# A two-layer backbone kernel: text and image tokens separated at two norm stages

## The reference

```python
for l in range(2):
    h_lat = modulate(rms_norm(x, g0), sh1, sc1)            # image tokens
    h_ctx = modulate(rms_norm(x_ctx, g0), csh1, csc1)      # text tokens
    if l == 0: y_lat, y_ctx = attention(h_lat, h_ctx) @ w_out
    else:      y_lat, _     = gated_delta_rule(h_lat, h_ctx) @ w_out
    x = x + gt1 * rms_norm(y_lat, g1)
    h = modulate(rms_norm(x, g2), sh2, sc2)
    x = x + gt2 * rms_norm((silu(h @ w_gate) * (h @ w_up)) @ w_down, g3)
    if l == 0: ...the same two updates for x_ctx with y_ctx and its own sh, sc, gt...
```

## Time and profile before

| | us |
|---|---|
| runs (3), median | 1237.39 (1236.99 to 1237.61) |
| the profiled execution | 1236.43 |
| its span in the trace | 1234.7 |
| PE busy | 1169.0 (95%) |
| DVE busy | 616.0 (50%) |
| ACT busy | 564.1 (46%) |
| mean granted TensorE clock | 0.986 |

### The profile page before, as it was taken

How to read it: one execution, slowest core, us unless ns; L and a number is a source line. 1 busy time by engine, 2 the same in 40 slices (tenths; PEclk the granted TensorE clock), 3 DMA queues, 4 the chain that set the end, 5 groups by cost and what they waited for, 6 DMA issues and landing times.

```text
span 1234.7 us, 17661 instructions
## 1 busy us (share of the span) xinstructions
PE 1169.0 (95%) x6999; PEld 911.7 (74%) x6999; DVE 616.0 (50%) x973; ACT 564.1 (46%) x1061; POOL 121.2 (10%) x117
## 2 busy tenths in 40 slices
PE   6899989999899999999999889999979998999997
PEld 2577735468378888888888638788869976888886
DVE  2532258763543233333222276489986525666653
ACT  2622247764462223323222274866355535766642
POOL 0030320110001111111000000010015100111100
PEclk9899999999999999999999999999979999999999
DMA  9754656653553333333333462234203032766661
GB/s 345 222 163 143 181 181 228 205 138 87 159 146 102 92 96 102 93 95 94 94 94 97 148 154 76 69 84 111 62 18 86 5 102 69 205 187 187 186 191 68
DMA packets 222892, 159.51 MB, mean 129 GB/s; under 512 B 14794, under 2 KB 191324, under 8 KB 222812
## 3 DMA queue, kind: packets, MB, share of 16 engines
q1 hardware_dynamic: 222032, 158.11, 43.2%
q10 hardware_dynamic: 780, 0.29, 0.1%
HBM read 157.33 MB, written 1.05 MB: 128 GB/s over the span
## 4 chain that ended last, share of the span: by engine, by line
PE 80%; DVE 9%; ACT 6%; issue 2%; DMA 1%; SPq 1%; POOL 0%; DVEq 0%; ACTq 0%; POOLq 0%
PE bank L1409 44%; PE bank L1420 6%; PE bank L1591 5%; PE bank L1421 3%; PE bank L1396 2%; PE bank L1467 2%; PE bank L1663 2%; PE bank L1498 1%; ACT h_work L1788 1%; PE bank L1673 1%; DVE blocks L1046 1%; DVE outer L1044 1%; PE bank L804 1%; PE bank L1517 1%; PE bank L1694 1%
## 5 line engine op out<-in xcount | busy, mean ns | idle before, releaser
L1409 PE MATMUL bank<-h_both,w_hi 128*128 128x512 f32 x1296 | 404.0, 393 | 0.0
L2002 DVE TENSOR_TENSOR w_lo<-w_raw,w_hi 128x1024 fp32r<-128x1024 f32 (+1 forms) x161 | 201.9, 1254 | 235.4 <-ACT w_hi L1755 234.4
L1409 PEld LDWEIGHTS bank<-h_both,w_hi 128*128 128x128 f32 x1296 | 242.0, 188 | 51.1 <-issue 0.7
L1409 PE MATMUL bank<-h_both,w_lo 128*128 128x512 f32 x648 | 252.5, 390 | 0.0
L1755 ACT ACTIVATE w_hi<-w_raw 128x1024 fp32r<-128x1024 f32 (+1 forms) x161 | 167.2, 1040 | 81.1 <-PE bank L1409 57.0
L1409 PEld LDWEIGHTS bank<-h_both,w_lo 128*128 128x128 f32 x648 | 121.6, 188 | 25.6
L1421 PE MATMUL bank<-h_both,w_lo 128*128 128x256 f32 x308 | 86.5, 281 | 0.0
L1420 PE MATMUL bank<-h_both,w_hi 128*128 128x512 f32 x231 | 83.0, 398 | 1.4 <-DVE h_both L2059 1.0
L1409 PE MATMUL bank<-act_hi,w_hi 128*128 128x512 f32 x176 | 68.5, 389 | 0.0
L1409 PE MATMUL bank<-act_lo,w_hi 128*128 128x512 f32 x176 | 68.5, 389 | 0.0
L1409 PE MATMUL bank<-act_hi,w_lo 128*128 128x512 f32 x176 | 68.5, 389 | 0.0
(11 more groups left out here) (301 smaller groups left out, 1834.0 us busy)
## 6 DMA issues: line engine op xcount, KB each, us to landing
w_raw<-in_ada_w SPq DMA_DIRECT2D x96, 512.0 KB, 4.8
w_raw<-in_ffn_w_gate_up SPq DMA_DIRECT2D x88, 512.0 KB, 3.9
w_raw<-in_ffn_w_down SPq DMA_DIRECT2D x38, 512.0 KB, 3.8
w_raw<-in_gdn_w_in SPq DMA_DIRECT2D x32, 512.0 KB, 4.0
w_raw<-in_attn_w_in SPq DMA_DIRECT2D x14, 512.0 KB, 4.0
w_raw<-in_gdn_w_out SPq DMA_DIRECT2D x8, 512.0 KB, 5.2
w_raw<-in_ffn_w_down SPq DMA_DIRECT2D x8, 384.0 KB, 3.4
w_raw<-in_attn_w_in SPq DMA_DIRECT2D x8, 256.0 KB, 3.4
```

The costliest lines, as they stand in the source:

```text
L1409: m = nc.tensor.matmul(dst, stationary(a, k), moving(b, k), start=(first and k == kk[0] and a == b == 0), stop=(last and k == kk[-1] and a ...
L2002: nc.vector.tensor_tensor(w_lo[where[key] % N_RAW][:, 0:tiles, 0:w], raw_slot(key)[:, 0:tiles, 0:w], w_hi[hi_slot(m)][:, 0:tiles, 0:w].bit ...
```

## The change

The streams get separate jobs and semaphores at two places. The attention output is made in two passes over its 8 tiles, first the text columns, then the image columns, with the text stream's norms put among the image tiles; five gate tiles (`HELD`) are then made for text columns, and then for image columns, each on its own PSUM bank, the image stream's norms among the text half. The last down tile is made text first and then image, and three delta rule tiles (`DELTA_HELD`: ab, k0, k1) likewise. All matmuls at these places, the norms' too, have 256 columns in place of 512. The weights of the tiles that are held need places: five spare `w_hi` slots lie where `act_hi` and the attention buffers are unused. Of the 11 ada chunks behind attention and the 11 behind the down tiles, 12 go in pairs behind the gate tiles 8, 14, 20, 26, 32 and 38, and 10 (2, 4 and 4) stay behind the down tiles. Helpers named `..._part` and `..._held` do for one stream what `take_y`, `sum_y`, `post_norm` and `pre_norm` did for both; `square_part` and `pre_step` keep the ring of 4 squares. In the diff, cut to its core, the PE program comes first, then `down_held` and `out_held` of ACT and of DVE.

```diff
-GAP_COUNTS = (2, 3, 6)
-ADA_GAPS = {"gap0": 34 + 2 * len(ADA_UNITS), "gap1": 34 + 2 * len(ADA_UNITS) + sum(GAP_COUNTS)}
+GAP_COUNTS = (2, 4, 4)
+ADA_GATES = [8 + 6 * n for n in range(6)]
+ADA_GAPS = {"gap1": 34 + 2 * len(ADA_UNITS) + 2 * len(ADA_GATES)}
...
+    if phase == "gate0" and step in ADA_GATES:
+        return pair(34 + 2 * len(ADA_UNITS), ADA_GATES.index(step))
...
-    out += [("attout", m) for m in range(KT)] + [("ada", a) for a in gap("gap0")]
+    out += [("attout", m) for m in range(KT)]
...
+        w_hi += [at(f"w_hi_spare{n}", [KT, P], F32R, BIG + 16384 + 4096 * n) for n in range(5)]
...
+        SPARE = {split_no["attout", m]: N_SPLIT + 1 + m - 3 for m in range(3, KT)}
+        SPARE.update({split_no["gdn", "k", n]: N_SPLIT - 1 + n for n in range(2, 4)})
+        SPARE.update({split_no["gate", 0, n]: N_SPLIT + 1 + n - 3 for n in range(3, HELD + 2)})
+        hi_slots, hi_users, last_user, turns = [], [], {}, 0
+        for n in range(len(split_chunks)):
+            j = (n - LATE) % (N_SPLIT + 1)
+            if n in SPARE:
+                slot = SPARE[n]
+            elif n < LATE:
+                slot = turns % N_SPLIT
+                turns += 1
+            else:
+                slot = (turns + j) % N_SPLIT if j < N_SPLIT else N_SPLIT
+            hi_slots.append(slot)
+            hi_users.append(last_user.get(slot, None))
+            last_user[slot] = n
...
+                if n >= WHOLE_AT:
                     project_whole(key)
-                elif n > 1:
+                elif n >= DELTA_HELD:
...
-                for m in range(KT):
-                    project(("attout", m), ("y", 0, m), 0, there=None if m else heads_there)
+                for s in range(2):
+                    for m in range(KT):
+                        w, job = weights(("attout", m)), y_job(0, m, s)
+                        finish(three(take(job)[:, token_cols(s)], w,
+                                     lambda part, k: (h_hi, h_lo)[part][:, k, token_cols(s)],
+                                     range(KT), True, True, before=heads_there if m == s == 0 else None), job)
+                        if s and m == 0:
+                            post_part(0, 0)
+                        if s and m == 4:
+                            pre_part(1, 0)
+            def post_part(i, s):
+                pe.wait_ge(y_acc_parts[s], acc_no(i, KT - 1, s))
+                dst = take(post_job(i, s), "side")
+                finish(nc.tensor.matmul(dst[:, token_cols(s)], ones, post_views[i][2][:, token_cols(s)],
+                                        start=True, stop=True), post_job(i, s))
+            def pre_step(j, s, k):
+                if k == 0:
+                    take(pre_job(j, s), "side")
+                pe.wait_ge(sq_parts[s], norm_no(j, k, s))
+                m = nc.tensor.matmul(bank(pre_job(j, s))[:, token_cols(s)], ones, pre_sq[:, k % 4, token_cols(s)],
+                                     start=(k == 0), stop=(k == KT - 1))
+                finish(m, ("held_sq", j, s, k))
+                done_at[pre_job(j, s)] = jobs[0]
+            def pre_part(j, s):
+                for k in range(KT):
+                    pre_step(j, s, k)
+            def held_step(j, dsts, ws, s, k):
+                pe.wait_ge(h_parts[s], norm_no(j, k, s))
+                for key in dsts:
+                    width = dsts[key].shape[0]
+                    for a, b in ((0, 0), (0, 1), (1, 0)):
+                        m = nc.tensor.matmul(dsts[key][:, token_cols(s)], ws[key](a, k)[:, 0:width],
+                                             (h_hi, h_lo)[b][:, k, token_cols(s)],
+                                             start=(k == a == b == 0), stop=(k == KT - 1 and a == 1))
+                    if s and k == KT - 1:
+                        finish(m, key)
+            def gates_held():
+                held = [("gate", 0, n) for n in range(HELD)]
+                dsts, ws = {}, {}
+                for keys in [held[0:2]] + [[key] for key in held[2:]]:
+                    for key in keys:
+                        dsts[key], ws[key] = take(key), weights(key)
+                    for k in range(KT):
+                        held_step(1, {key: dsts[key] for key in keys}, ws, 0, k)
+                        if keys[0] == held[0] and k == 1:
+                            post_part(0, 1)
+                    if keys[0] == held[HELD - 2]:
+                        pre_part(1, 1)
+                for k in range(KT):
+                    held_step(1, dsts, ws, 1, k)
+            def delta_held():
+                held = [("gdn",) + GDN_STEPS[n] for n in range(DELTA_HELD)]
+                dsts = {key: take(key, "gdn")[0:chunk_shape(key)[1]] for key in held}
+                ws = {key: weights(key) for key in held}
+                for k in range(KT):
+                    held_step(2, dsts, ws, 0, k)
+                    if k >= 2:
+                        pre_step(2, 1, k - 2)
+                for k in range(KT - 2, KT):
+                    pre_step(2, 1, k)
+                for k in range(KT):
+                    held_step(2, dsts, ws, 1, k)
+            def last_down():
+                m = KT - 1
+                keys = [("down", 0, m, part) for part in range(len(DOWN_PARTS))]
+                ws = [weights(key) for key in keys]
+                for s in range(2):
+                    job = y_job(1, m, s)
+                    dst = take(job)[:, token_cols(s)]
+                    for part, (a, b) in enumerate(DOWN_PARTS):
+                        last = three(dst, lambda p, k: ws[part](p, k - a),
+                                     lambda p, k: (act_hi, act_lo)[p][:, k, token_cols(s)],
+                                     range(a, b), part == 0, part == len(DOWN_PARTS) - 1)
+                        finish(last, keys[part] if s else ("downc", m, part))
+                        if s and part == 0:
+                            post_part(1, 0)
+                    done_at[job] = jobs[0]
+                ada(ada_after("gap1", 0))
+                post_part(1, 1)
+                ada(ada_after("gap1", 1))
+                pre_part(2, 0)
+                ada(ada_after("gap1", 2))
...
-            ada(ada_after("gap0", 0))
-            post_norm(0)
-            ada(ada_after("gap0", 1))
-            pre_norm(1)
-            ada(ada_after("gap0", 2))
             ffn(0)
-            ada(ada_after("gap1", 0))
-            post_norm(1)
             if LAST_SUB == 3:
-                ada(ada_after("gap1", 1))
-                pre_norm(2)
-                ada(ada_after("gap1", 2))
+                delta_held()
...
+            def down_held():
+                take_part(1, KT - 1, 0)
+                post_part(1, 0)
+                for k in range(KT):
+                    square_part(2, k, 0)
+                    if k == 3:
+                        take_part(1, KT - 1, 1)
+                    if k == 5:
+                        post_part(1, 1)
+                first = split_no["gdn", "ab", 0]
+                split_to(first + 1)
+                pre_part(2, 0)
+                def squares(k):
+                    if k < KT:
+                        square_part(2, k, 1)
+                    if k == 0:
+                        split_to(first + 2)
+                h_part(2, 0, squares)
+                pre_part(2, 1)
+                def steps(k):
+                    if k in (4, 7):
+                        split_to(first + DELTA_HELD + k // 7)
+                h_part(2, 1, steps)
+            def out_held():
+                for m in range(KT):
+                    split_out(split_to, 0, m)
+                    take_part(0, m, 0)
+                take_part(0, 0, 1)
+                post_part(0, 0)
+                take_part(0, 1, 1)
+                for k in range(3):
+                    square_part(1, k, 0)
+                take_part(0, 2, 1)
+                for k in range(3, 4):
+                    square_part(1, k, 0)
+                split_gate(split_to, 0)
+                take_part(0, 3, 1)
+                take_part(0, 4, 1)
+                for k in range(4, KT):
+                    square_part(1, k, 0)
+                split_gate(split_to, 1)
+                pre_part(1, 0)
+                def other(k):
+                    if k in (1, 4, 7):
+                        take_part(0, 5 + k // 3, 1)
+                h_part(1, 0, other)
+                split_gate(split_to, 2)
+                post_part(0, 1)
+                split_gate(split_to, 3)
+                for k in range(KT):
+                    square_part(1, k, 1)
+                    if k == 3:
+                        split_gate(split_to, 4)
+                pre_part(1, 1)
+                def gates(k):
+                    if k == KT - 2:
+                        split_gate(split_to, HELD)
+                h_part(1, 1, gates)
+                split_gate(split_to, HELD + 1)
...
+            def down_held():
+                sum_part(1, KT - 1, 0)
+                def last_sum(k):
```

(51 more changed lines are left out.)

147 lines of the change are left out of this document (121 added, 26 removed).

## The result

The changed kernel takes 1251.03 us (median of 4 runs, 1250.5 to 1252.41), the kernel before beside it 1237.22 (4 runs, 1236.99 to 1237.61): a ratio of 1.0113, 95% interval 1.0098 to 1.0128. It is slower by 13.8 us, on the side that I forecast, but 11 us above the forecast and 6.5 above the range. The profiled executions stand further apart than the medians, 1252.41 against 1236.43 us.

The account below looks back on a forecast made before the run. PE's matmuls bound the kernel, except behind attention and the down tiles, where an ACT and DVE latency chain does. 1236.43 - 7.0 (attention, net) + 8.7 (down tiles) + 0.9 (clock) = 1239.0 profiled, 1240.0 us as median; range 1232.0 to 1244.5.

Parts of the forecast that it names:

- Clock: Behind attention and the down tiles: one fall to half clock loses 1.7 us; half of one was counted, 0.9 us.
- two falls 3.4: Clock case within the forecast's side: two falls, each over a PE-bound stretch, cost 3.4 us in place of 0.9, giving 1242.5.
- Work behind the down tiles: From the end of down tile 6 to `cum`, PE's work without waits was counted as 51.9 us.
- Waits behind the down tiles: From the end of down tile 6 to `cum`, seven listed PE waits were to come to 19.4 us together.
- the ring: Behind the down tiles: ACT's image squares 4 to 7 wait for PE's `pre_step` on the 4-deep ring; 1.5 us in all.
- ab's copy: Behind the down tiles: PE waits for the copy of ab before its transpose, 0.8 us.
- wait 3: Before the first held delta rule matmul, PE waits for late k0 and k1 DMAs, their copies and the text chain: 6.9 us.
- Behind attention: From attention's output tiles to the end of gate 4: gain of 12.9 us, with no PE wait over 1 us.
- Moved ada chunks: Twelve ada chunks moved between gate tiles, where PE is always busy: 6 pairs at 0.98 us, 5.9 us lost.
- Start: Attention's output tiles were taken to start at 274.44 us, as in the kernel before.
- its 7.8: Lower value of the loss behind the down tiles, with half-width matmuls at 0.1133 us instead of 0.118.
- The rival "faster": Behind the down tiles wait 3 is short, text h follows 5.5 us earlier and the clock stays up: 1233.6 us; chance 0.20.

Follow-up runs that it names:

- e3: Changed kernel plus idle matmuls, never read, ahead of TensorE's four long waits behind the down tiles; 1244.11 us.
- e5: Changed kernel with its half behind the down tiles undone and VectorE's order there as in the kernel before; 1228.98 us.
- e6: Changed kernel with five ada chunks run early on TensorE, ahead of the last down tile; 1251.39 us.
- e9: Changed kernel with the first three delta rule chunks right behind two ada chunks in SyncE's queue, and eight ada pairs among the gate tiles; 1252.20 us.
- e2: Changed kernel with attention's end put back as in the kernel before, streams parted only behind the down tiles; 1261.89 us.
- e12: Changed kernel with two delta rule tiles held, k1's copies in the image half, last down weights requested late, idle matmuls in two long waits; 1240.09 us.
- e10: Changed kernel with two delta rule tiles held instead of three, and k1's copies moved into the image half; 1244.84 us.

## Why the prediction was wrong

To the Gram start the loss is 810.63 - 795.64 = 15.0 us, the prediction's sum 8.7 + 0.9 - 7.0 = 2.6. The 12.4 us between, by its steps:

- **Clock: the step that failed, 8.4 us.** "I count half of one fall, 0.9 us" and "two falls 3.4" at worst. There were four stretches, 23.8 us, each behind a wait of 2.2 us or more; the work under them cost 9.3 us by the estimate above, 5.9 ahead of `cum` and 3.4 behind it. Filling the waits gave back 7.7 (e3). The prediction had a row of the kernel before with waits of up to 3 us at 1.00 and took it for a rule. But e5, with nearly the same waits in that place, falls there twice (706.9 and 720.5 us). It costs nothing there: from the end of tile 7 to `cum` e5 takes 46.6 us, and so does the kernel before, because ScalarE and VectorE lead. And the kernel before has a second fall behind attention, from 340.0 us, behind a wait of 2.5 us, which the prediction passed over (window, PE only):

```profile
340.00:342.00 2.00, 2.00 (x5) 0.50 1.10 286
```

- **Work behind the down tiles, 1.4 us.** Counted 51.9. PE is busy for 59.2 there; 5.9 of the difference are the half clock, 0.6 the spacing of 0.120 in place of 0.118. The other 0.8 I can't place.
- **Waits behind the down tiles, -1.0 us.** 18.4 against 19.4, each at its place: 3.3 (3.1), 8.5 (6.9), 3.4 before the image half (4.2 with k2's copy), 2.2 (2.4), 0.3 (0.5), 0.6 on the ring (1.5), and nothing for ab's copy (0.8). For wait 3 the prediction named both causes, the slots eight back and the order on ScalarE and VectorE; e6 and e9 show both, and that neither mends it alone. What it had not seen is that the queue hangs on the last down tile's held weights, not only on the ada chunks.
- **Behind attention, 1.5 us.** 84.4 us from attention's first tile to the end of gate 4, against 82.9: the spacing was at the upper bound or just over it (23.63/195 and 14.66/120, 0.121 and 0.122), and 624 x 0.002 = 1.2. (The prediction's own terms, 355.8 + 0.2 + 0.4 + 0.7, give 357.1 and not 357.3.) Gain 11.4 instead of 12.9. No wait over 1 us, as said.
- **Moved ada chunks, 1.4 us.** The 0.98 of the row is the piece; each pair also breaks the row of gate matmuls. 324.2 us less 1398 x 0.2267 leaves 7.3, or 1.22 a pair.
- **Start, 0.6 us.** Attention's tiles began at 275.04 in place of 274.44.

Together 12.3 of the 12.4 us. One of the prediction's bounds was also added up wrong, and moves nothing: 276 matmuls at 0.1133 save 1.3 us, so its 7.8 should be 7.4.

Behind the Gram start another 0.9 us came, with a longer half-clock stretch in the scan (17.1 us in place of 13.7). The forecast's side and its reason, more lost behind the down tiles than won behind attention, were right, and e5 and e2 show it: -3.9 and +20.4 us. The rival "faster" needed wait 3 to be short, and it was the longest.

The attention half alone, e5, beats both kernels: 1228.98 us, 22 less than the changed kernel and 9.0 less than the one before. With three repairs of its second half together (e12) the changed kernel stays 7.4 us behind e5 at the Gram start.

## What to carry to other kernels

Price a new wait of a matmul-bound engine twice: its length, and the matmuls behind it at half clock. Here four waits of 2.2 to 8.5 us cost 17 us by themselves, and filling them gave back 7.7 more. The second price is a risk and not a sure cost: waits of the same length brought the clock down in one kernel and not in another, so one row at full clock is no promise. Where a tile's weights must be held over two passes, look at what an in-order queue has behind their slots: the queue stood 15.5 us, and reordering TensorE's work did not free it. And try the parts of a change singly: up to the Gram matmuls one half won 3.9 us and the other lost 18.9.

## What was not expected of the hardware

- Idle matmuls make the kernel faster: 36 of 0.43 us, never read, gave 6.9 us, and 18 of them in one wait took away the fall that stood behind it (granted clock 1.00 where it was 0.50) and no other.
- The length of a wait did not tell whether the clock would fall. Behind the 3.3 us ahead of down tile 7 it was 0.50 from 687.2 to 690.6 in the changed kernel and 1.00 in e9 and e10. Behind waits of 2.3 and 2.5 us behind attention the kernel before fell, and behind 2.3 and 2.1 us behind its down tiles it did not.
- The clock can be low under unbroken work for longer than the wait that it follows: behind one of 2.2 us, 6.8 us of `cum` and k3 at 0.50.
- The same work took 200.4 to 205.2 us from the Gram matmuls to the output tile, with issue gaps of 2.3 to 6.2 us in it, and with 10.2 to 17.1 us at half clock.
